# A two-layer hybrid encoder trunk on one core: the eight gate features computed with the tokens as the stationary side

## Chip, cores and metric

One Trainium2 chip, one core. The metric is the device time of one execution in microseconds (us).

## What is computed

The input x is 512 tokens by 1024 features in float32. Layer 0 normalises x (RMSNorm), projects it with one weight matrix and feeds two groups of heads: four gated DeltaNet heads and four differential-attention heads. Layer 1 is a banded attention. Each layer ends with a gated MLP. The part that the change touches is the projection of the DeltaNet gates: two numbers per head and token, a and b, so eight columns of the weight matrix in all.

```
h = rmsnorm(x, even_norm_mix[e])
dn_qkv, dn_a, dn_b, dn_gate, fq, fk, fv = split_cols(h @ even_w_in[e], IN0_SPLITS)
...
beta = jax.nn.sigmoid(b)
g = -jnp.exp(A_log) * jax.nn.softplus(a + dt_bias)
```

The recurrence of the DeltaNet needs beta and the running sums of g in every chunk, so nothing of the DeltaNet past its convolutions can start before them.

## The kernel before, in words

Every large product is made in a split form. A float32 operand is written as head plus tail, both in the float32r type: ScalarE rounds it to the head (`wh` for a weight, `mh` for the normalised input without its token scale), VectorE subtracts to get the tail (`wl`, `ml`). A product is then three matmuls, head by head, tail by head and head by tail, which add up in PSUM. The 1024 features are eight blocks of 128 (KD = 8), the 512 tokens four blocks of 128 (NB = 4). In the generator `features` (line 668 issues the matmul) a 128x128 block of a weight is stationary and all 512 tokens move past it; eight blocks times three forms, 24 matmuls, make one tile of 128 output features, and two tiles are one unit: tile 0 and tile 1 of slot 0 (banks acc0, acc1), then of slot 1 (acc2, acc3).

The first unit of each slot feeds DeltaNet heads 0 and 1. TensorE's order around the change is written out by hand: half of tile 0, the row sums of the norm (`norm_rows`), and so on, three matmuls at each step of `run`. Before the change it is: tile 0 and tile 1 of slot 0; `ab_features`; tile 0 of slot 1; `ab_tokens`; tile 1 of slot 1; then `dn_pair(0, ...)`, which begins with sums over the squares of q and k (`token_sums`, line 690) and later mixes its own small matmuls with further units.

`ab_features` computes the gate features as rows: for each of the eight blocks, three matmuls (`mm3`, lines 625 to 627) with a stationary side of 128x8 (`abh`, `abl`) and 512 moving tokens, into rows 0 to 7 of bank R2. VectorE copies these rows to SBUF (line 1785, into a slice of the tile U of head 1, which the profile calls dn_U). `ab_tokens` turns the rows into columns by four transposes (line 735) into bank R3: tokens on the partitions, eight features per token block. VectorE then multiplies by the token scale `rcol` (line 1798, `abz`) and begins a chain of small steps, in which each waits for the one before it (`chain`, lines 1802 to 1819), with five small ScalarE steps between (lines 1290 to 1295). They end in `gall` (g) and `ball` (beta).

VectorE works through its own list in a fixed order too: the convolutions of q and k of head 0 (lines 1519 to 1531), the copy of line 1785, the two halves of a weight tail (line 1540, after ScalarE's head, line 390), the gate chain, the convolutions of q and k of head 1, again a weight tail, and then the start of `dn_pair`. Each convolution begins by reading its finished tile (`tile_full`), so q of head 1 needs tile 0 of slot 1 and k of head 1 needs tile 1 of slot 1.

Of the kernel before, what the change touches and what calls it, by code (L numbers as in the profile page):

```python
# [25 lines left out]
F32 = mybir.dt.float32  # L26
R32 = mybir.dt.float32r
ALU = mybir.AluOpType
ACT = mybir.ActivationFunctionType

P = 128
S = 512
NB = S // P
D = 1024
KD = D // P
# [69 lines left out]
                                                  ("t31", 3), ("pv", 3)]  # L105
XT_JOBS = [(f"x{k}", k % 4) for k in range(KD)]
NORM_JOBS = [("col", 1), ("row", 0)]
AB_JOBS = [("abT", 2), ("ab", 3)]


class Bank:
# [19 lines left out]
BANK.phase("xt", XT_JOBS, 1)  # L131
BANK.phase("ab", AB_JOBS, 1)
BANK.phase("norm0", NORM_JOBS[1:], 1)
# [33 lines left out]
def build(nc, T, out):  # L167

    ctx = ExitStack()
    with ctx:  # L170
        def sb(name, shape, dt=F32, where=ctx):
            return where.enter_context(nc.sbuf_tensor(name, shape, dt))
# [3 lines left out]
        def sem(name):  # L176
            if name not in sems:
                sems[name] = ctx.enter_context(nc.semaphore(name))
            return sems[name]
# [13 lines left out]
        mh = sb("mh", [P, KD, S], R32)  # L193
        ml = sb("ml", [P, KD, S], R32)
# [3 lines left out]
        cst = sb("cst", [P, C_WIDTH])  # L198
# [13 lines left out]
        rcol = sb("rcol", [P, NB])  # L212
# [9 lines left out]
        abz = sb("abz", [P, NB, 8], F32, ctx)  # L222
# [6 lines left out]
        nq = sb("nq", [P, 2, NB], F32, ctx)  # L229
        sub8 = sb("sub8", [P, 1])  # L230
        abw = sb("abw", [P, KD, 8])
        abh = sb("abh", [P, KD, 8], R32)
        abl = sb("abl", [P, KD, 8], R32)
        sb("line2", [P, LINE])

        def cblk(n):
# [14 lines left out]
        start = ExitStack()  # L251
# [8 lines left out]
        d = [{}, {}]  # L260
# [23 lines left out]
            vn.append(sb(f"vn{h}", [P, P], F32, mix))  # L284
            st.append(sb(f"st{h}", [P, P], F32, mix))
        mix.close()
        abs_ = d[1]["U"][0:8, :]
        mixer = ExitStack()
        oh = sb("oh", [P, KD, S], R32, mixer)
        ol = sb("ol", [P, KD, S], R32, mixer)  # L290
# [56 lines left out]
        def full(eng, phase, job, i):  # L347

            b, n = BANK.use(phase, job, i)
            eng.wait_ge(sem(f"R{b}_full"), n + 1)  # L350
            return R[b]

        def free(ins, phase, job, i):

            b, _ = BANK.use(phase, job, i)
            ins.then_inc(sem(f"R{b}_read"), 1)

        def read(eng, phase, job, i):

            b, n = BANK.use(phase, job, i)  # L360
            eng.wait_ge(sem(f"R{b}_read"), n + 1)
# [251 lines left out]
        def _(pe):  # L613
            def job(phase, name, i, first=True):
                b, n = BANK.use(phase, name, i)
                if not (isinstance(n, int) and n == 0):
                    pe.wait_ge(sem(f"R{b}_read"), n)
                return R[b]

            def done(ins, phase, name, i):  # L620
                b, _ = BANK.use(phase, name, i)
                ins.then_inc(sem(f"R{b}_full"), 1)

            def mm3(o, ah_, al_, bh_, bl_, first, last):
                nc.tensor.matmul(o, ah_, bh_, start=first, stop=False)
                nc.tensor.matmul(o, ah_, bl_, start=False, stop=False)
                return nc.tensor.matmul(o, al_, bh_, start=False, stop=last)

            HEADS = (True, True)

            def features(s, g, mov, tiles=2, kn=KD, norm=None, ready=None, halves=None):
# [46 lines left out]
            def both(a, b):  # L678
                yield from a
                yield from b  # L680

            def run(gen, n=1000):
                for _ in range(n):
                    if next(gen, 0) == 0:
                        return
# [23 lines left out]
            for k in range(KD):  # L709
                r = job("xt", f"x{k}", 0)  # L710
                for b in range(NB):
                    last = nc.tensor.transpose(r[:, b * P:(b + 1) * P], xin[:, b, k * P:(k + 1) * P], ident)
# [5 lines left out]
            for t, n in ((1, 110), (2, 66)):  # L718
                last = nc.tensor.transpose(acc[1][:, t * P:t * P + n], prow[0:n, t, :], cst[0:n, 0:n])
            last.then_inc(sem("pv_full"), 1)  # L720

            def ab_features():

                pe.wait_ge(sem("ab_split"), 1)
                r = job("ab", "abT", 0)
                for k in range(KD):
                    last = mm3(r[0:8, :], abh[:, k, :], abl[:, k, :], mh[:, k, :], ml[:, k, :], k == 0, k == KD - 1)
                done(last, "ab", "abT", 0)

            def ab_tokens():  # L730

                read(pe, "ab", "abT", 0)
                r = job("ab", "ab", 0)
                for b in range(NB):
                    last = nc.tensor.transpose(r[:, b * 8:b * 8 + 8], abs_[:, b * P:(b + 1) * P], cst[0:8, 0:8])
                done(last, "ab", "ab", 0)


# [324 lines left out]
            first = both(features(0, 0, (mh, ml), norm=0), features(1, 0, (mh, ml)))  # L1063
            run(first, KD)
            pe.wait_ge(sem("cst_rest"), 16)
            norm_rows(0)
            run(first, KD)
            ab_features()
            run(first, KD)
            ab_tokens()  # L1070
            run(first)

# [28 lines left out]
            first = both(features(0, UNIT["odd"], (mh, ml), norm=2), features(1, UNIT["odd"], (mh, ml), tiles=1))  # L1101
# [22 lines left out]
            for k in range(KD):  # L1124
                r = job("yt", f"x{k}", 0)
                pe.wait_ge(sem("x_gain"), k + 1)
                for b in range(NB):
                    last = nc.tensor.transpose(r[:, b * P:(b + 1) * P], x[:, k, b * P:(b + 1) * P], ident)
# [4 lines left out]
        def _(act):  # L1133
            A = nc.scalar.activation
# [49 lines left out]
                A(mh[:, k, :], xs[:, k, :], ACT.Copy, scale=pv[:, k:k + 1]).then_inc(sem("m_head"), 1)  # L1184
            units_split_act(act, 1, 0)
            act.wait_ge(sem("abw_in"), 16)
            A(abh[:, :, :], abw[:, :, :], ACT.Copy).then_inc(sem("ab_head"), 1)


            def silu(i, c, dst):  # L1190
# [93 lines left out]
            first = qk_evac(0)  # L1284
# [175 lines left out]
        def _(dve):  # L1460
            V = nc.vector
# [24 lines left out]
            for k in range(KD):  # L1486
                r = full(dve, "xt", f"x{k}", 0)
# [8 lines left out]
            for t, n in ((1, 110), (2, 66)):  # L1496
                ins = V.tensor_copy(pv[:, t * P:t * P + n], acc[1][:, t * P:t * P + n])  # L1497
            ins.then_inc(sem("pv_copied"), 1)
            for k in range(1, KD):
# [1 line left out]
            norm_rstd(0)  # L1501
            units_split_dve(dve, 1, 0)
            dve.wait_ge(sem("ab_head"), 1)
            V.tensor_tensor(abl[:, :, :], abw[:, :, :], abh[:, :, :].bitcast(F32), ALU.subtract)\
                .then_inc(sem("ab_split"), 1)
            dve.wait_ge(sem("pv_copied"), 2)
            V.tensor_scalar(sub8[:, :], pv[:, PV_SUB:PV_SUB + 1], 1.0 - LAM_INIT, None, ALU.mult).then_inc(step, 1)
# [37 lines left out]
            def qk_evac(p):  # L1545
                for h in (0, 1):
                    for c in (0, 1):
                        yield conv(2 * p + h, c, 0)
                        yield conv(2 * p + h, c, 1)
                    yield from half_splits(h, 2 * p + 1)  # L1550
# [230 lines left out]
            first = qk_evac(0)  # L1781
            for _ in range(4):
                next(first, 0)
            r = full(dve, "ab", "abT", 0)
            free(V.tensor_copy(abs_[:, :], r[0:8, :]), "ab", "abT", 0)
            for _ in range(2):
                next(first, 0)

# [2 lines left out]
            def chain(ins):  # L1791
                n_step[0] += 1
                ins.then_inc(step, 1)
                dve.wait_ge(step, n_step[0])


            r = full(dve, "ab", "ab", 0)
            ins = V.tensor_tensor(abz[:, :, :], r[:, 0:NB * 8].rearrange("p (b n) -> p b n", n=8),
                                  rcol[:, :].unsqueeze(2).broadcast_to([P, NB, 8]), ALU.mult)
            free(ins, "ab", "ab", 0)  # L1800
            read(dve, "ab", "ab", 0)
            chain(V.tensor_tensor(abt[0][:, :, :], abz[:, :, 0:4], dtb[:, :].unsqueeze(1).broadcast_to([P, NB, NH]),
                                  ALU.add))
            chain(V.tensor_tensor(lt[:, :, :], lp[:, :].rearrange("p (a b n) -> p a b n", a=2, b=2)[:, :, 0, :],
# [238 lines left out]
            for k in range(KD):  # L2043
                r = full(dve, "yt", f"x{k}", 0)
# [27 lines left out]
```

## Time and profile before

| | |
|---|---|
| median of 3 runs | 1423.88 us |
| lowest and highest run | 1422.25 and 1428.67 us |
| the profiled execution's own time | 1423.34 us |
| its span in the trace | 1421.7 us |
| TensorE (PE) busy | 1365.0 us, 96% of the span |
| TensorE weight loads (PEld) busy | 1120.1 us, 79% |
| VectorE (DVE) busy | 827.9 us, 58% |
| ScalarE (ACT) busy | 582.4 us, 41% |
| GpSimd (POOL) busy | 131.9 us, 9% |
| mean granted TensorE clock | 0.981 of full |

The profiled execution ran 1.6 us longer than its span, which lies around the traced instructions. The busy share is an average over stages with different limits: it says that TensorE works nearly always, not that a given matmul sets the end. For a change in one place the chain of waits and the timeline of that place decide. A timeline row gives start, length, engine, line, operation, and in brackets the idle time before it and what ended it. Lengths of matmuls overlap, so the pace of a stream is read from the starts of its rows.

### The profile page before, as it was taken

Reading aid. Unit: us, or ns where it says so; the run is one execution under the profiler, and the core shown is the slowest. Engines: PE = TensorE matmul, PEld = TensorE weight load, DVE = VectorE, ACT = ScalarE, POOL = GpSimd, SP = SyncE. Lnnn points to the kernel's source line nnn. Section 1 sums busy time; section 2 is a strip of 40 time slices with the busy share of each in tenths; the row PEclk is TensorE's granted clock in tenths of the full one; section 3 lists DMA queues with packets and bytes.
Section 4 is the critical chain, followed back from the end, with each engine's and each line's share of the span. In section 5 each row is a group of like instructions: output and inputs, shape, how many; then the busy total and the mean of one; then the engine's idle time right before and its main releaser. Section 6 shows DMA issues by size and latency. Waiting matters only on the chain.

```text
span 1421.7 us, 19249 instructions
## 1 busy us (share of the span) xinstructions
PE 1365.0 (96%) x6871; PEld 1120.1 (79%) x6871; DVE 827.9 (58%) x1243; ACT 582.4 (41%) x804; POOL 131.9 (9%) x141
## 2 busy tenths in 40 slices
PE   5799999999899999999999999999999999999996
PEld 4689889777678888888888777777878888888885
DVE  5685685677475665345655555555655654355543
ACT  4423322355444443223334455554435442233342
POOL 1050040011041100000001100100210000000011
PEclk9899899999999999999999999999999999999998
DMA  7411110124144533343223432233223333433132
GB/s 205 139 30 30 45 27 19 45 60 129 35 128 132 164 101 89 96 118 89 77 74 104 113 88 73 72 91 100 59 81 97 90 94 89 114 93 110 55 93 59
DMA packets 218643, 124.77 MB, mean 88 GB/s; under 512 B 6047, under 2 KB 215434, under 8 KB 218340
## 3 DMA queue, kind: packets, MB, share of 16 engines
q1 hardware_dynamic: 213744, 112.48, 28.1%
q0 software_dynamic: 3664, 11.58, 2.9%
q8 instruction: 31, 0.51, 0.2%
q10 hardware_dynamic: 1188, 0.08, 0.1%
q14 instruction: 16, 0.13, 0.0%
HBM read 119.87 MB, written 9.48 MB: 91 GB/s over the span
## 4 chain that ended last, share of the span: by engine, by line
PE 92%; DVE 4%; ACT 2%; DMA 1%; issue 1%; SPq 0%; POOL 0%; DVEq 0%; ACTq 0%; POOLq 0%
PE acc L668 73%; PE R L784 5%; PE acc L1029 3%; PE R L898 2%; PE R L912 2%; PE R L1002 1%; PE R L690 1%; DVE wl L394 1%; PE R L782 1%; PE R L772 1%; ACT wh L390 1%; PE R L961 1%; DMA xin<-in_x 1%; DVE cta L1531 1%; DVE ml L1481 1%
## 5 line engine op out<-in xcount | busy, mean ns | idle before, releaser
L668 PE MATMUL acc<-mh,wh 128*128 128x512 f32 x1120 | 318.1, 404 | 5.4 <-DVE pv L1497 4.6
L668 PE MATMUL acc<-ml,wh 128*128 128x512 f32 x1120 | 308.6, 393 | 3.1 <-DVE ml L1481 3.1
L668 PE MATMUL acc<-mh,wl 128*128 128x512 f32 x1120 | 308.2, 394 | 0.0
L394 DVE TENSOR_TENSOR wl<-raw,wh 128x2048 fp32r<-128x2048 f32 (+1 forms) x104 | 224.4, 2157 | 118.2 <-ACT wh L390 118.2
L390 ACT ACTIVATE wh<-raw 128x2048 fp32r<-128x2048 f32 x112 | 202.5, 1808 | 130.2 <-PE acc L668 128.8
L668 PEld LDWEIGHTS acc<-mh,wh 128*128 128x128 f32 x1120 | 205.9, 189 | 57.2 <-issue 15.7
L668 PEld LDWEIGHTS acc<-ml,wh 128*128 128x128 f32 x1120 | 209.4, 189 | 48.8 <-DVE ml L1481 4.6
L668 PEld LDWEIGHTS acc<-mh,wl 128*128 128x128 f32 x1120 | 210.4, 189 | 43.4
L529 POOL TENSOR_TENSOR ssum<-ssum,sq 128x512 f32<-128x512 f32 x32 | 49.9, 1560 | 733.5 <-ACT sq L1143 732.9
L1993 DVE SCALAR_TENSOR_TENSOR cta<-cb,pv,cta 128x512 f32<-128x512 f32 x88 | 66.2, 752 | 74.1 <-ACT cta L1420 67.7
L668 PE MATMUL acc<-ah,wh 128*128 128x512 f32 x352 | 95.4, 389 | 0.0
L668 PE MATMUL acc<-al,wh 128*128 128x512 f32 x352 | 95.4, 389 | 0.0
L668 PE MATMUL acc<-ah,wl 128*128 128x512 f32 x352 | 95.4, 389 | 0.0
L1420 ACT ACTIVATE cta<-cb,pv 128x512 f32<-128x512 f32 x44 | 35.9, 817 | 103.8 <-DVE cb L1986 103.6
L668 PEld LDWEIGHTS acc<-ah,wh 128*128 128x128 f32 x352 | 66.1, 188 | 13.7
L668 PEld LDWEIGHTS acc<-al,wh 128*128 128x128 f32 x352 | 66.1, 188 | 13.7
L668 PEld LDWEIGHTS acc<-ah,wl 128*128 128x128 f32 x352 | 66.1, 188 | 13.7
L2013 DVE TENSOR_TENSOR x<-x,acc 128x512 f32 (+1 forms) x32 | 22.0, 688 | 70.6 <-PE acc L668 69.9
L1426 ACT ACTIVATE ah<-pd 128x512 f32 x44 | 27.8, 632 | 69.6 <-DVE pd L2002 69.6
L2004 DVE TENSOR_TENSOR al<-pd,ah 128x512 f32 x44 | 30.5, 692 | 44.3 <-ACT ah L1426 44.3
L1424 ACT ACTIVATE sl<-cta 128x512 f32<-128x512 f32 x44 | 27.8, 632 | 64.8 <-DVE cta L1993 64.8
L1842 DVE CUSTOM_DVE_ANT_0 odd_ns<-R,gb 128x128 f32<-128x128 f32 (+3 forms) x64 | 28.8, 487 | 37.3 <-PE R L898 37.3
(308 smaller groups left out, 1624.1 us busy)
## 6 DMA issues: line engine op xcount, KB each, us to landing
raw<-in_ffn_w_in SPq DMA_DIRECT2D x88, 512.0 KB, 5.0
raw<-in_even_w_in SPq DMA_DIRECT2D x24, 512.0 KB, 5.3
raw<-in_ffn_w_out SPq DMA_DIRECT2D x32, 384.0 KB, 4.1
raw<-in_ffn_w_out SPq DMA_DIRECT2D x32, 320.0 KB, 3.7
raw<-in_odd_w_qkv SPq DMA_DIRECT2D x16, 512.0 KB, 4.5
rel_bias_extended<-rel_bias_rows POOLq DMA_DIRECT2D x16, 320.0 KB, 4.0
raw<-in_even_w_out SPq DMA_DIRECT2D x8, 512.0 KB, 4.6
raw<-in_odd_w_qkv SPq DMA_DIRECT2D x16, 256.0 KB, 3.1
```

The source lines that it names most:

```text
L390: nc.scalar.activation(wh[s][:, 0:n], raw[s][:, 0:n], ACT.Copy).then_inc(sem(f"w_head{s}"), 1)
L394: nc.vector.tensor_tensor(wl[s][:, 0:n], raw[s][:, 0:n], wh[s][:, 0:n].bitcast(F32), ALU.subtract).then_inc(sem(f"w_tail{s}"), 1)
L529: pool.tensor_tensor(ssum[:, :], ssum[:, :], sq[s][:, :], ALU.add).then_inc(sem("ssum"), 1)
L668: last = nc.tensor.matmul(acc[2 * s + t][:, :], ws[0 if form[0] else 1][:, t, k, :], mov[0 if form[1] else 1][:, k, :], start=form == HEAD ...
L784: last = nc.tensor.matmul(r[:, t], a[:, t], triu if b is triu else b[:, t], start=True, stop=True)
L898: ins = nc.tensor.matmul(r[m][:, w], qs[x_][half[m], b * P:(b + 1) * P], ks[y][half[m], w], start=(step == 0), stop=(step == 2))
L912: last = nc.tensor.transpose(r[:, c0 + k * P:c0 + (k + 1) * P], src[:, k * P:(k + 1) * P], ident)
L1029: ins = nc.tensor.matmul(acc[2 * s + t][:, :], ws[0 if form[0] else 1][:, t, k, :], (oh if form[1] else ol)[:, k, :], start=form == HEADS ...
L1420: A(cta[s][:, :], cb[s][:, ALPHA - 2:ALPHA - 2 + S], ACT.Identity, bias=pv[:, bass.ds(j + (PV_CB + JF * layer), 1)], scale=pv[:, bass.ds(j ...
L1842: free(V.tensor_tensor_reduce(out=dst[t % 2][:, 0:w], in0=R[t % 2][:, 0:w], in1=bias, scale=-1.0, scalar=3e38, op0=ALU.add, op1=ALU.min, a ...
L1993: V.scalar_tensor_tensor(out=cta[s][:, :], in0=cb[s][:, o:o + S], scalar=pv[:, bass.ds(j + (w0 + JF * tap), 1)], in1=cta[s][:, :], op0=ALU ...
L2004: V.tensor_tensor(dyn(al, 2 * i + s), pd[s][:, :], dyn(ah, 2 * i + s).bitcast(F32), ALU.subtract).then_inc(sem("a_tail"), 1)
```

## The change

The stationary and the moving side are swapped. A 128x128 block of `mh` or `ml` (128 features by 128 tokens) is stationary, and the weight columns move: the head and the tail of the eight columns stand side by side in one tile `abx` of 16 columns per block. `mh` takes all 16 (head by head and head by tail at once, into two groups of 8 columns of PSUM), `ml` the first 8. This gives 4 token blocks x 8 feature blocks x 2 = 64 matmuls with the tokens on the partitions already, so the copy of line 1785 and the four transposes go. The two groups of columns are added on VectorE. `ab_features` is gone, and `ab_tokens` stands where it stood, ahead of tile 0 of slot 1.

```diff
-AB_JOBS = [("abT", 2), ("ab", 3)]
+AB_JOBS = [("ab", 3)]
...
-        abh = sb("abh", [P, KD, 8], R32)
-        abl = sb("abl", [P, KD, 8], R32)
+        abx = sb("abx", [P, KD, 16], R32)
...
-            def ab_features():
-
-                pe.wait_ge(sem("ab_split"), 1)
-                r = job("ab", "abT", 0)
-                for k in range(KD):
-                    last = mm3(r[0:8, :], abh[:, k, :], abl[:, k, :], mh[:, k, :], ml[:, k, :], k == 0, k == KD - 1)
-                done(last, "ab", "abT", 0)
-
             def ab_tokens():
 
-                read(pe, "ab", "abT", 0)
+                pe.wait_ge(sem("ab_split"), 1)
+                pe.wait_ge(sem("m_tail"), KD)
                 r = job("ab", "ab", 0)
                 for b in range(NB):
-                    last = nc.tensor.transpose(r[:, b * 8:b * 8 + 8], abs_[:, b * P:(b + 1) * P], cst[0:8, 0:8])
+                    t = slice(b * P, (b + 1) * P)
+                    for k in range(KD):
+                        nc.tensor.matmul(r[:, b * 16:b * 16 + 16], mh[:, k, t], abx[:, k, :],
+                                         start=(k == 0), stop=False)
+                        last = nc.tensor.matmul(r[:, b * 16:b * 16 + 8], ml[:, k, t], abx[:, k, 0:8],
+                                                start=False, stop=(k == KD - 1))
                 done(last, "ab", "ab", 0)
...
             run(first, KD)
-            ab_features()
-            run(first, KD)
             ab_tokens()
             run(first)
...
-            r = full(dve, "ab", "abT", 0)
-            free(V.tensor_copy(abs_[:, :], r[0:8, :]), "ab", "abT", 0)
...
             r = full(dve, "ab", "ab", 0)
-            ins = V.tensor_tensor(abz[:, :, :], r[:, 0:NB * 8].rearrange("p (b n) -> p b n", n=8),
-                                  rcol[:, :].unsqueeze(2).broadcast_to([P, NB, 8]), ALU.mult)
+            parts = r[:, 0:NB * 16].rearrange("p (b a n) -> p b a n", a=2, n=8)
+            chain(V.tensor_copy(abz[:, :, :], parts[:, :, 0, :]))
+            ins = V.tensor_tensor(abz[:, :, :], abz[:, :, :], parts[:, :, 1, :], ALU.add)
             free(ins, "ab", "ab", 0)
             read(dve, "ab", "ab", 0)
+            chain(V.tensor_tensor(abz[:, :, :], abz[:, :, :], rcol[:, :].unsqueeze(2).broadcast_to([P, NB, 8]), ALU.mult))
```

ScalarE writes the head into `abx[:, :, 0:8]` in place of `abh`, and VectorE the tail into `abx[:, :, 8:16]` in place of `abl`, each at the same place in its list.

TensorE's list around the gate features, before the change (acc are the tiles of the projection, R the bank of the gate features; the second number of a stationary or output shape is the moving side's columns):

```order
L668 MATMUL acc<-ml,wh 128x512 x4
L625 MATMUL R<-mh,abh 8x512
L626 MATMUL R<-ml,abh 8x512
L627 MATMUL R<-mh,abl 8x512
...
L668 MATMUL acc<-mh,wh 128x512 x4
...
L735 MATMUL R<-cst,dn_U 128x8 x4
L668 MATMUL acc<-mh,wh 128x512 x4
```

And after it:

```order
L661 MATMUL acc<-ml,wh 128x512 x4
L723 MATMUL R<-abx,mh 128x16
L725 MATMUL R<-abx,ml 128x8
...
L661 MATMUL acc<-mh,wh 128x512 x4
L661 MATMUL acc<-ml,wh 128x512 x4
L661 MATMUL acc<-mh,wl 128x512 x4
```

The pair of lines 723 and 725 comes 32 times in a row where the triple of lines 625 to 627 came 8 times; the transposes that stood between tile 0 and tile 1 of slot 1 are gone.

VectorE's list from the last convolution of head 0 to the start of the gate chain, before:

```order
L1531 SCALAR_TENSOR_TENSOR cta<-cb,pv,cta 128x512 x3
L1785 COPY dn_U<-R 8x512
L1540 TENSOR_TENSOR wl<-raw,wh 128x1024 x2
L1798 TENSOR_TENSOR abz<-R,rcol 128x32
L1802 TENSOR_TENSOR abt<-abz,dtb 128x16
```

And after:

```order
L1520 SCALAR_TENSOR_TENSOR cta<-cb,pv,cta 128x512 x3
L1529 TENSOR_TENSOR wl<-raw,wh 128x1024 x2
L1786 COPY abz<-R 128x32
L1787 TENSOR_TENSOR abz<-abz,R 128x32
L1790 TENSOR_TENSOR abz<-abz,rcol 128x32
L1791 TENSOR_TENSOR abt<-abz,dtb 128x16
```

One instruction of 512 columns is gone ahead of the weight tail, and one instruction has become three behind it. Nothing else changes its place.

## Rows read from the trace of the kernel before

**Rows 1.** The page: busy time of TensorE, and the chain that ended last.
```profile
PE 1365.0 (96%) x6871; PEld 1120.1 (79%) x6871; DVE 827.9 (58%) x1243; ACT 582.4 (41%) x804; POOL 131.9 (9%) x141
...
PE 92%; DVE 4%; ACT 2%; DMA 1%; issue 1%; SPq 0%; POOL 0%; DVEq 0%; ACTq 0%; POOLq 0%
```

**Rows 2.** The chain in order of time (start us, us, what), around the gates.
```profile
46.02 0.36 PE R L735 x4
...
51.62 0.70 DVE cb L1519
...
55.30 0.70 DVE cb L1519
...
62.55 2.36 DVE wl L1540 x2
...
65.37 2.08 PE R L784 x8
```

**Rows 3.** Timeline of TensorE, 34.9 to 60.8 us (start, length, engine, line).
```profile
34.88 0.40 PE L625 MATMUL R<-mh,abh 128*8 128x512 f32 x1
...
40.42 1.07 PE L668 MATMUL acc<-mh,wh 128*128 128x512 f32 x4
...
45.95 0.41 PE L735 MATMUL R<-cst,dn_U 8*128 8x8 f32 x4
...
50.96 1.07 PE L668 MATMUL acc<-mh,wl 128*128 128x512 f32 x4
51.87 0.94 PE L690 MATMUL R<-cst,dn_sqq 128*128 128x1 f32 x8
...
60.77 1.87 PE L690 MATMUL R<-cst,dn_sqq 128*128 128x1 f32 x8 [7.07 <-ACT dn_sqk L1206]
```

**Rows 4.** Timeline of VectorE, 40.6 to 46.8 us.
```profile
40.62 0.68 DVE L1785 COPY dn_U<-R 8x512 f32<-8x512 f32 x1 [0.65 <-PE R L627]
43.66 2.36 DVE L1540 TENSOR_TENSOR wl<-raw,wh 128x1024 fp32r<-128x1024 f32 x2 [2.36 <-ACT wh L390]
46.40 0.19 DVE L1798 TENSOR_TENSOR abz<-R,rcol 128x32 f32<-128x32 f32 x1 [0.38 <-PE R L735]
46.62 0.17 DVE L1802 TENSOR_TENSOR abt<-abz,dtb 128x16 f32<-128x16 f32 x1
```

**Rows 5.** Timeline of TensorE at two stretches of one moving column per 128x128 stationary side.
```profile
172.13 3.55 PE L690 MATMUL R<-cst,dn_A 128*128 128x1 f32 x16
175.55 2.05 PE L784 MATMUL R<-cst,dn_decT 128*128 128x128 f32 x8
...
272.71 1.84 PE L690 MATMUL R<-cst,dn_A 128*128 128x1 f32 x16
274.48 0.33 PE L898 MATMUL R<-ksh,qsh 64*128 64x128 f32 x2
```

**Rows 6.** Stretches: length, busy us of PE, PEld, DVE, ACT, POOL, then granted clock, DMA.
```profile
168.70:175.50 6.80, 6.80 (x32) 6.80 (x33) 4.92 (x12) 4.76 (x7) 0.00 (x0) 0.50 0.21 49
...
34.90:40.40 5.50, 5.50 (x25) 2.19 (x24) 4.79 (x7) 1.03 (x2) 0.00 (x0) 1.00 1.13 395
21.40:24.80 3.40, 3.40 (x8) 2.75 (x9) 3.40 (x6) 3.38 (x5) 0.00 (x0) 0.50 1.03 268
54.00:55.40 1.40, 0.00 (x0) 0.00 (x0) 1.26 (x3) 0.17 (x1) 0.00 (x0) 1.00 0.00 0
55.60:60.70 5.10, 0.00 (x0) 0.00 (x0) 3.13 (x5) 2.02 (x5) 0.00 (x0) 0.50 0.00 0
...
69.00:69.50 0.50, 0.50 (x5) 0.50 (x5) 0.47 (x2) 0.00 (x0) 0.00 (x0) 0.80 1.19 289
```

**Rows 7.** Timeline of TensorE, the first wide matmuls after a pause, at the lower clock.
```profile
21.39 2.02 PE L668 MATMUL acc<-mh,wh 128*128 128x512 f32 x4 [4.57 <-DVE pv L1497]
23.21 1.84 PE L668 MATMUL acc<-mh,wl 128*128 128x512 f32 x4
24.88 1.09 PE L668 MATMUL acc<-ml,wh 128*128 128x512 f32 x4
```

More of the change, by code:

```diff
@@ L286, in build @@
         mix.close()
-        abs_ = d[1]["U"][0:8, :]
         mixer = ExitStack()
@@ L622, in done @@
                 ins.then_inc(sem(f"R{b}_full"), 1)
[L624 to L627, printed above, removed]
             HEADS = (True, True)
@@ L720, in _, with ab_tokens @@
             last.then_inc(sem("pv_full"), 1)
-            def ab_features():
+            def ab_tokens():
                 pe.wait_ge(sem("ab_split"), 1)
-                r = job("ab", "abT", 0)
-                for k in range(KD):
-                    last = mm3(r[0:8, :], abh[:, k, :], abl[:, k, :], mh[:, k, :], ml[:, k, :], k == 0, k == KD - 1)
-                done(last, "ab", "abT", 0)
-            def ab_tokens():
-                read(pe, "ab", "abT", 0)
+                pe.wait_ge(sem("m_tail"), KD)
                 r = job("ab", "ab", 0)
                 for b in range(NB):
-                    last = nc.tensor.transpose(r[:, b * 8:b * 8 + 8], abs_[:, b * P:(b + 1) * P], cst[0:8, 0:8])
+                    t = slice(b * P, (b + 1) * P)
[4 more added lines that the diff above has]
+                                                start=False, stop=(k == KD - 1))
                 done(last, "ab", "ab", 0)
@@ L1186, in _ @@
             act.wait_ge(sem("abw_in"), 16)
-            A(abh[:, :, :], abw[:, :, :], ACT.Copy).then_inc(sem("ab_head"), 1)
+            A(abx[:, :, 0:8], abw[:, :, :], ACT.Copy).then_inc(sem("ab_head"), 1)
             def silu(i, c, dst):
@@ L1503, in _ @@
             dve.wait_ge(sem("ab_head"), 1)
-            V.tensor_tensor(abl[:, :, :], abw[:, :, :], abh[:, :, :].bitcast(F32), ALU.subtract)\
+            V.tensor_tensor(abx[:, :, 8:16], abw[:, :, :], abx[:, :, 0:8].bitcast(F32), ALU.subtract)\
                 .then_inc(sem("ab_split"), 1)
```

## Prediction

> **What bounds the kernel now.** I read the page first: TensorE is busy 96% of the span and carries 92% of the chain that ended last [rows 1]. So a microsecond taken from TensorE counts in most places, and I next asked whether it counts here. The chain in order of time [rows 2] shows TensorE until the four transposes end at 46.38, and then VectorE and ScalarE: the gate chain, the two convolutions of head 1 (51.62 and 55.30), a weight tail at 62.55, and TensorE again only at 65.37. The timeline of TensorE [rows 3] agrees: after the last wide matmul, issued before 51.87, and sixteen one-column ones it sits idle for 7.07 us until 60.77. So TensorE's work between 35 and 53 us is bound only through the places where VectorE waits for it. From the dense part behind 65 us on TensorE leads, so a delay of VectorE here comes out whole at the end.
>
> The timeline of VectorE [rows 4] shows how thin the first of these places is. The copy of line 1785 ends at 41.30, and VectorE then idles 2.36 us until ScalarE's weight head arrives. The weight tail ends at 46.02, and the gate chain begins at 46.40, 0.38 us later, released by the transposes. So all that TensorE and the copy do for the gates before the change costs the end 0.38 us.
>
> **What goes.** On TensorE 24 matmuls of 512 columns, from 34.88 to 40.42, are 5.5 us, and the four transposes, 45.95 to about 46.3, are 0.4 us [rows 3]. On VectorE the copy of 0.68 us lies in idle time [rows 4] and is worth nothing; without it VectorE would idle from 40 to 43.66 for the same weight head. ScalarE's list is the same. No DMA moves: the loads of SyncE wait for weight tails, and these keep their time.
>
> **What comes on VectorE.** Three small instructions in a row where one was. One step of this kind, with the wait for its forerunner, is 0.22 us by the starts 46.40 and 46.62 [rows 4]. If the gates are in PSUM in time, the first starts at 46.02, and line 1791 would start at 46.02 + 3 x 0.22 = 46.68, against 46.62 for the same step before: 0.06 us later. The 0.38 us won are given back. The new order puts the gates' bank ahead of tile 0 of slot 1, so this needs the 64 matmuls to end before 46.0. The new wait for the eight `m_tail` costs nothing: those tails were needed by the tiles ahead, long done.
>
> **What comes on TensorE.** 64 matmuls, each with its own 128x128 stationary side and 16 or 8 moving columns. The trace has no float32r matmul of this shape. The nearest rows are the sums of line 690, also a 128x128 stationary side each time, with one moving column: 16 of them take 274.48 - 272.71 = 1.77 us, 0.111 us each, at the upper clock, and 175.55 - 172.13 = 3.42 us, 0.214 us each, at the lower one [rows 5]. The bound above is the wide stream itself, which swaps such a side for each matmul: four take 51.87 - 50.96 = 0.91 us, 0.228 each at the upper clock [rows 3]. I take line 690's prices, since the shape is almost the same: 64 x 0.111 = 7.1 us, against 5.5 + 0.4 removed, or 64 x 0.214 = 13.7 us. One matmul costs half of a wide one, but there are 64 for 24.
>
> For the loads a rule speaks against the change in the same size. The Trainium skill, "TensorE: Matmul & The Clock Gate", section "LDWEIGHTS (loading the stationary operand)", prices a load by its columns over 1.2: 107 ns for 128 columns, so an estimate of 6.8 us for 64, and 7 ns for 8 columns. The trace's 0.111 us agrees; the sum does not use the page's figure.
>
> **The clock.** This decides the sign. Which price holds hangs on the granted clock. In the stretch 168.70 to 175.50 TensorE is busy all of 6.80 us with one-column matmuls, and the clock stands at 0.50, the lower level (1.2 GHz), throughout [rows 6]: this work did not lift it. After the last wide matmul before 51.87 the clock was still 1.00 (the upper level, 2.4 GHz) until 55.4 and 0.50 from 55.6 on, and the first 1.8 us of that were one-column matmuls [rows 3, 6]. The removed block, 34.90 to 40.40, ran at 1.00 [rows 6] because it was itself wide. I therefore expect the clock to fall inside the new block. Where, the rows leave open; I take half of the matmuls at each level: 32 x 0.111 + 32 x 0.214 = 10.4 us, with 7.1 and 13.7 as the ends.
>
> The wide matmuls behind it then start low. After the pause at 21.39 the first eight took 24.88 - 21.39 = 3.49 us, 0.436 each [rows 7], 0.21 more than at the upper clock. Eight of them cost 1.7 us.
>
> **The sum.** Block from 34.9 to 45.3. Gates in time for 46.0. Tile 0 of slot 1, 24 wide matmuls, 5.5 + 1.7 = 7.2 us, to 52.5; the convolution of q of head 1 wants it at 51.6 and starts 1.0 us late. Tile 1, 5.5 us, to 58.0, its end 0.1 later. The convolution of k of head 1 wanted it at 55.30 [rows 2], and with q's delay alone would start at 56.3; it starts at 58.1, **2.8 us late**. Behind it stand, on VectorE and ScalarE one after the other, the silu, the squares, ScalarE's weight head, the weight tail at 62.55 and the first work of the pair at 65.37; all of them move by it. Against the profiled execution's 1423.3 this gives 1426.1. That execution is 0.5 us below the median of the three runs. The ends: with 7.1 us the block ends at 42.0 and tile 1 at 53.1, before 55.3, so nothing is late and the time is 1423.3 (the 0.06 us of VectorE is below what can be seen). With 13.7 us it ends at 48.6, the gates are late by 2.3 us, tile 1 ends at 61.4, and k's convolution is 6.1 us late: 1429.4. The clock rises again only at about 69 [rows 6], with the path on TensorE since 65.37; if that rise shifts, it may add or take 1 to 2 us (at half speed, 3.8 us of work would shrink by 1.9).
>
> A difference under 0.5%, 7.1 us, is what a measurement of this kernel hardly tells from none. All of this lies inside it.
>
> **Rival 1: the clock holds (chance 0.35).** The block takes 7.1 us at 1.00, TensorE's idle time before 60.77 shrinks by 1.2 us, and the end is where it was: 1423.3. For it speaks that TensorE is never without work in the block, and that 16 moving columns are more than one. Against it stands the stretch from 168.70 [rows 6]. The Trainium skill, same page, section "Why this matters for your kernels", advises to keep TensorE busy to reach and hold the upper clock; by that rule the clock holds here and the time is that of this rival. The trace disagrees where the work is one-column matmuls: busy 6.80 of 6.80 us at 0.50.
>
> **Rival 2: a float32r side is not swapped faster than the wide stream shows (chance 0.05, of it 0.04 for the slow form).** The wide rows never show a swap below 0.228 us at the upper and 0.436 at the lower clock, since the 512 columns cover it; line 690's sides are of float32 in two passes and could differ. With half of the matmuls at each clock the block takes 32 x 0.228 + 32 x 0.436 = 21.2 us and ends at 56.1, tile 1 at 68.9, and k's convolution is 13.6 us late: 1436.9, slower than before beyond doubt. With the clock up throughout, 14.6 us, tile 1 ends at 60.6: 1428.6. With the clock low behind the block, the loss passes 7.1 us when tile 1 ends after 62.4, so when the block ends after 49.6: 14.7 us, or 0.230 us for one matmul on average. Against it: weight loads of the wide stream and of line 690 look alike in length, and nothing in the rows ties a swap to the type.
>
> **Rival 3: TensorE leaves the chain and the end comes earlier (chance 0.05, of it 0.01 beyond 0.5%).** The chain lists the 24 matmuls and the transposes, some 5.9 us, and whoever reads only that list expects them back. The 0.38 us of [rows 4] is all that can come before the weight tail holds, and the two added steps take 0.44. The time would be 1423.3 - 0.3 = 1423.0 if the steps overlap better than their starts say; with the pair's start at the upper clock too, 1.9 less, 1421.1.
>
> **How the numbers follow.** My forecast, a clock that falls in the block, has a chance of 0.55, and its own range is 1423.5 to 1429.5. The range reaches down over rivals 1 and 3 to 1422.0, the price of a run's spread below 1423.3 (the lowest of the three was 1422.25), and up to the end with all 64 at the lower clock. Slower by over 0.5% needs rival 2's slow form, 0.04. Faster by over 0.5% has 0.01. The rest, 0.95, is within it.
>
> **What would show it.** In the trace of the changed kernel: 64 matmuls starting near 34.9, their pace 0.11 us and, from some point on, 0.21; the granted clock 0.50 by the end of the block; the next wide matmuls at 0.44 for some three microseconds; the copy of line 1786 starting near 46.0, ended by no wait for TensorE; the convolution of k of head 1 waiting for TensorE for about 2 us and starting near 58; the idle time of TensorE before the squares of head 1 still about 6 to 7 us; and the first work of the pair (line 784 in the kernel before) near 68 in place of 65.4. The prediction is wrong in its main step if the clock stays at 1.00 through the block, if the pace at the upper clock is not near 0.11, or if k's convolution does not wait for tile 1. It would be wrong as a whole if a delay there did not come out at the end, so if a later stall shrank by it.

## Result, and the profile after

The changed kernel took 1432.51 us in the median of 8 runs (1423.91 to 1434.01), the kernel before 1425.43 us in 8 runs (1421.23 to 1430.66). The ratio is 1.0050, 95% interval 1.0030 to 1.0069: slower, by 7.1 us in the medians, where 2.8 us were forecast and a range up to 1429.5. Both kernels spread over some 10 us. Between executions of one kernel the time goes with the mean granted clock of TensorE: of the kernel before, executions at 0.983 took 1421 to 1423 us and those at 0.976 to 0.977 about 1428 to 1430 (by the 98 runs of it beside the experiments). The changed kernel has such a split too: seven of its eight runs took 1430.8 to 1434.0 us at 0.972 to 0.975, and one took 1423.91 us at 0.980.

The page of the profiled execution (span 1431.3 us, against 1421.7) shows that TensorE is busy 12.9 us longer while VectorE and ScalarE do the same as before [rows 1]:

```profile
span 1431.3 us, 19321 instructions
PE 1377.9 (96%) x6907; PEld 1134.7 (79%) x6907; DVE 828.5 (58%) x1244; ACT 582.3 (41%) x804; POOL 132.0 (9%) x141
```

The timeline of TensorE through the block and behind it answers to [rows 3, 7]. The columns are start, length, engine, line, what, shapes:

```profile
30.34 1.02 PE L696 MATMUL R<-sq,cst 128*128 128x512 f32 x2
...
36.69 0.17 PE L723 MATMUL R<-abx,mh 128*128 128x16 f32 x1
...
37.05 0.26 PE L723 MATMUL R<-abx,mh 128*128 128x16 f32 x1
37.16 0.25 PE L725 MATMUL R<-abx,ml 128*128 128x8 f32 x1
...
43.56 0.36 PE L723 MATMUL R<-abx,mh 128*128 128x16 f32 x1
43.77 0.35 PE L725 MATMUL R<-abx,ml 128*128 128x8 f32 x1
...
46.12 2.05 PE L661 MATMUL acc<-mh,wh 128*128 128x512 f32 x4
47.97 1.91 PE L661 MATMUL acc<-ml,wh 128*128 128x512 f32 x4
49.68 1.88 PE L661 MATMUL acc<-mh,wl 128*128 128x512 f32 x4
51.39 1.10 PE L661 MATMUL acc<-mh,wh 128*128 128x512 f32 x4
```

The pace is 0.11 us at first and 0.21 us later. The block takes 46.12 - 36.69 = 9.4 us, with about 40 of the 64 matmuls at the fast pace and 24 at the slow one. The twelve wide matmuls behind it take 5.27 us in place of 2.7, 2.5 us more. This execution had already been 1.8 us later at the row sums of the norm (line 696, in the kernel before line 703 at 28.54), ahead of anything the change touches. The kernels below whose lists are as before up to there start it anywhere between 28.5 and 30.6, so I count from this row on.

The granted clock (third number from the end, as in [rows 6]) says the same:

```profile
36.70:41.10 4.40, 4.40 (x42) 4.40 (x40) 4.12 (x7) 0.63 (x1) 0.00 (x0) 1.00 1.12 364
41.20:46.10 4.90, 4.90 (x25) 4.90 (x25) 1.22 (x2) 4.24 (x5) 0.00 (x0) 0.50 0.62 264
46.20:51.30 5.10, 5.10 (x13) 4.03 (x13) 3.58 (x11) 1.84 (x6) 1.98 (x5) 0.50 0.49 128
...
69.90:78.60 8.70, 8.70 (x33) 7.93 (x34) 5.66 (x15) 3.65 (x9) 0.00 (x0) 0.50 0.48 121
78.70:100.00 21.30, 21.30 (x108) 16.84 (x107) 17.08 (x24) 4.60 (x5) 9.57 (x7) 1.00 0.00 1
```

It is 1.00 for the first 4.4 us of the block and 0.50 for the rest and for the first wide matmuls. The last two rows belong to the first pair, to which I come back.

The timeline of VectorE, against [rows 4], and the convolutions of head 1 against [rows 2]:

```profile
45.45 2.36 DVE L1529 TENSOR_TENSOR wl<-raw,wh 128x1024 fp32r<-128x1024 f32 x2 [3.68 <-ACT wh L388]
47.73 0.18 DVE L1786 COPY abz<-R 128x32 f32<-128x32 f32 x1
47.95 0.19 DVE L1787 TENSOR_TENSOR abz<-abz,R 128x32 f32<-128x32 f32 x1
48.17 0.19 DVE L1790 TENSOR_TENSOR abz<-abz,rcol 128x32 f32<-128x32 f32 x1
48.40 0.17 DVE L1791 TENSOR_TENSOR abt<-abz,dtb 128x16 f32<-128x16 f32 x1
...
54.39 0.69 DVE L1508 TENSOR_TENSOR cb<-acc,rstd 128x512 f32<-128x512 f32 x1 [0.81 <-PE acc L661]
...
59.77 0.69 DVE L1508 TENSOR_TENSOR cb<-acc,rstd 128x512 f32<-128x512 f32 x1 [1.81 <-PE acc L661]
```

The copy starts as the weight tail ends, without a wait; the gate chain's first own step (line 1791) stands at 48.40, and less the 1.8 us this is 46.60, where it was 46.62. Tile 0 of slot 1 comes 0.8 us late and tile 1 another 1.8. In the kernel before both waits were absent. TensorE's pause before the squares of head 1, 7.07 us before the change [rows 3], is now 3.83 us:

```profile
65.25 1.87 PE L683 MATMUL R<-cst,dn_sqq 128*128 128x1 f32 x8 [3.83 <-ACT dn_sqk L1195]
```

**The ledger.** The start of the same TensorE instructions in the two profiled executions, and their difference. The first work of pair 0 in the kernel before is the 65.37 of [rows 2]:

| place | before | after | difference |
|---|---|---|---|
| row sums of the norm | 28.54 | 30.34 | +1.80 |
| pair 0, first work (line 784, now 775) | 65.37 | 69.85 | +4.48 |
| pair 0, first spread (line 772, now 763) | 72.74 | 79.56 | +6.82 |
| pair 1, first work | 175.55 | 182.27 | +6.72 |
| pair 1, first spread | 184.07 | 192.07 | +8.00 |
| sums behind pair 1 (line 690, now 683) | 272.71 | 280.71 | +8.00 |
| values of the first attention head (line 907, now 898) | 281.07 | 290.69 | +9.62 |
| span | 1421.7 | 1431.3 | +9.6 |

So 1.8 us is the later start, 2.7 us is what the block does by way of VectorE, and 2.3, 1.3 and 1.6 us come at three later places where the code is the same. In all three the clock is low in the changed kernel where it was up before. Before, it had risen at 69.00 to 69.50 [rows 6]; after, at 78.7. At the last of them it falls once more:

```profile
282.96 1.62 PE L661 MATMUL acc<-mh,wh 128*128 128x512 f32 x4
284.38 1.91 PE L661 MATMUL acc<-ml,wh 128*128 128x512 f32 x4
286.09 1.48 PE L661 MATMUL acc<-mh,wl 128*128 128x512 f32 x4
```

The same three rows in the kernel before started at 274.96, 275.98 and 276.88, so twelve wide matmuls took 4.4 us here and 2.8 us there. These are differences of two single executions, 1432.98 and 1423.34 us; the medians are 7.1 us apart.

### The profile page after: what moved, and what is told of

Same layout as the page of the kernel before. It is cut to its first block, busy times and chain, and to the rows that moved or that the text cites. A ratio compares the mean times of both kernels' runs of the same rounds, so it can differ in the third digit from the quotient of the medians.

```text
span 1431.3 us, 19321 instructions
## 1 busy us (share of the span) xinstructions
PE 1377.9 (96%) x6907; PEld 1134.7 (79%) x6907; DVE 828.5 (58%) x1244; ACT 582.3 (41%) x804; POOL 132.0 (9%) x141
## 4 chain that ended last, share of the span: by engine, by line
PE 93%; DVE 3%; ACT 2%; DMA 1%; issue 1%; SPq 0%; POOL 0%; DVEq 0%; ACTq 0%; POOLq 0%
PE acc L661 73%; PE R L775 5%; PE acc L1020 3%; PE R L889 2%; PE R L903 2%; PE R L993 1%; PE R L683 1%; PE R L773 1%; PE R L763 1%; ACT wh L388 1%; PE R L952 1%; DMA xin<-in_x 1%; DVE wl L392 1%; DMA out<-ob 0%; PE R L878 0%
## 5 line engine op out<-in xcount | busy, mean ns | idle before, releaser
L661 PE MATMUL acc<-ml,wh 128*128 128x512 f32 x1120 | 312.4, 397 | 3.1 <-DVE ml L1470 3.1
```

Source lines behind the costliest of these rows:

```text
L661: last = nc.tensor.matmul(acc[2 * s + t][:, :], ws[0 if form[0] else 1][:, t, k, :], mov[0 if form[1] else 1][:, k, :], start=form == HEAD ...
```

## Experiments

Two questions. Is it the clock that makes the block long (theory A) or the 64 loads (B)? And are the 4 to 5 us behind the first pair chance (L), a fixed price of a later start (P, G), or a price that depends on where the start falls (Q)? Each kernel ran beside the kernel before on the same chip. Experiments 1 to 4, 5 to 8 and 9 to 12 are three groups, with their own runs of the kernel before (medians 1423.72, 1423.37 and 1423.74 us). The ratio with its 95% interval is an estimate of its own and not the quotient of the two medians. With these spreads the two can differ: in experiment 7 the medians are 3.0 us apart, while the ratio of 1.0004 is 0.6 us. So 2 or 3 us between medians are not much to build on. "Pair start" is the first work of pair 0 (line 784 of before) minus the row sums of the norm, 36.83 us in the kernel before and 39.51 in the changed one. It comes from one profiled execution, the time from the medians.

**1. Passing the columns eight times.**

```diff
-nc.tensor.matmul(r[:, b * 16:b * 16 + 16], mh[:, k, t], abx[:, k, :], ...)
+nc.tensor.matmul(r[:, b * P:(b + 1) * P], mh[:, k, t],
+                 abx[:, k, :].unsqueeze(1).broadcast_to([P, 8, 16]), ...)
...
```

The matmul of `ml` gets its 8 columns eight times over in the same way.

> The changed kernel, with the same 64 stationary loads, but the 16 (and 8) weight columns are passed eight times over, so that 128 (and 64) columns move past each load; the gate features come out eight times and one set is read. Theory A (the block's narrow matmuls let the clock fall, and the fall is the price): the granted clock stays 1.00 from 34 us to 55 us, the pace is 0.11 us for each of the 64, the block takes 7.1 us, k's convolution of head 1 waits for no matmul, and the median is within 2 us of the kernel before. Theory B (the 64 loads themselves are the price): the block still runs at 0.15 us or more on average, 9.4 us or more, and the time stays 5 us or more above before.

1431.57 against 1423.72 us, ratio 1.0053 (1.0037 to 1.0069): no better. The clock was not held:

```profile
35.10:38.50 3.40, 3.40 (x33) 3.40 (x31) 3.19 (x5) 0.63 (x1) 0.00 (x0) 1.00 1.19 362
38.60:45.30 6.70, 6.70 (x34) 6.70 (x33) 2.96 (x4) 4.86 (x5) 0.52 (x1) 0.50 0.59 253
```

Half of the block again ran at 0.50, with 128 and 64 columns behind each load. My expectation was wrong: eight times the columns did not save it. It does not speak for B, since the loads at 1.00 kept a pace of 0.11 us; it says that this remedy does not reach the clock.

The profiled execution of this kernel took 1423.67 us, the fastest of its twelve. It is worth a look, because its delay is that of the changed kernel: k's convolution waits 1.81 us and the pair start is 39.54. But here the clock rises at 72.7, 4.4 us after the pair's first work, where it was 8.8 us in the changed kernel's profile:

```profile
68.28 2.07 PE L778 MATMUL R<-cst,dn_decT 128*128 128x128 f32 x8 [1.03 <-DVE dn_decT L1636]
...
73.08 1.17 PE L661 MATMUL acc<-mh,wh 128*128 128x512 f32 x4
74.09 1.08 PE L661 MATMUL acc<-ml,wh 128*128 128x512 f32 x4
```

Counted from the row sums, its first attention head comes 3.1 us later than in the kernel before; in the changed kernel's profile that was 7.8 us. (By its end this execution is level with the kernel before's profiled one, which was low from 424.2 to 427.5 us where this one was not.) So the same delay brings some 5 us more behind it in one execution and almost nothing in another. Of the 32 runs of the changed kernel and of experiments 1 and 9, which share its delay, seven took 1423.3 to 1426.9 us and the others 1430.8 to 1434.3.

**2. The block in four groups.**

```diff
 for b in range(NB):
     ...16 matmuls of token block b...
+    if b == NB - 1:
+        done(last, "ab", "ab", 0)
+    run(first, 2)
```

> The changed kernel, its 64 matmuls in four groups of 16 with 6 wide matmuls behind each. Theory A: wide matmuls never stop for more than 1.8 us, the clock stays 1.00, tile 0 of slot 1 ends at 35+7.1+5.5 = 47.5 us and tile 1 at 53, before k's convolution wants it; time as before, within 2 us. Theory B: 2.7 us or more above before, as in the changed kernel.

```profile
36.80:54.90 18.10, 18.10 (x113) 16.15 (x112) 11.26 (x27) 8.79 (x13) 1.91 (x5) 1.00 0.69 225
```

The clock stays 1.00 through all 64, their 7.1 us and the 48 wide matmuls among and behind them. k's convolution waits for nothing (57.76, right behind q's). The pair start is 37.36, 0.53 us later than before, because the last group ends just late for the gate chain, which waits 0.27 us and has two more steps. The median is 1425.82, 2.1 us above before, ratio 1.0011 (0.9995 to 1.0026): just at the 2 us of theory A and not told from no difference. So A holds for the block: the same 64 loads, with the clock up, cost VectorE 0.5 us in place of 2.7.

**3. Half of the block.** Only `mh` is stationary; the tail of the input is left out of the gate features.

```diff
-nc.tensor.matmul(r[:, b * 16:b * 16 + 8], ml[:, k, t], abx[:, k, 0:8], ...)
```

> The changed kernel without the 32 matmuls of ml: the tail of the input is left out of the gate features. Theory A: 32 narrow matmuls take 3.6 us at 0.111 us, end before the clock falls or just as it falls; tile 1 of slot 1 ends near 50 to 51 us and k's convolution waits for nothing, so the time is within 1 us of before if nothing else moves. If the clock still falls, behind the block, the wide matmuls pay 1.7 us but tile 1 is ready at 52: still no wait.

```profile
35.23 3.63 PE L723 MATMUL R<-abx,mh 128*128 128x16 f32 x32
38.72 1.80 PE L661 MATMUL acc<-mh,wh 128*128 128x512 f32 x4
40.32 1.91 PE L661 MATMUL acc<-ml,wh 128*128 128x512 f32 x4
```

32 matmuls in 3.5 us, and the clock falls just behind them. The wide matmuls pay for it, yet tile 1 is in time, the pair start is 36.93 and the median 1423.88 against 1423.72 (0.9988 to 1.0021). A low clock where TensorE has slack was free here.

**4 to 6. A later pair start and nothing else.** The kernel before, with extra VectorE work ahead of k's convolution of head 1:

```diff
+for late in (d[0]["U"], d[1]["U"], d[0]["A2"], d[1]["A2"], ...)[:n]:   # n is 2, 4 or 6
+    V.tensor_tensor(late, rstd[:, :], rstd[:, :], ALU.mult)
```

Four instructions:

> The kernel before, with four extra VectorE instructions (about 2.5 us, results unused) ahead of k's convolution of head 1, so the first pair starts about 2.5 us later and TensorE's matmuls are all as before. The changed kernel's profiled run lost 2.7 us there and 5.1 us more at three later places, where the clock rose later or fell once more. Theory L (the later losses are chance of the execution): median 2 to 3 us above before. Theory P (a later start of the pair by itself brings the later rises): median 5 to 8 us above before.

Six:

> The kernel before with six extra VectorE instructions (about 3.7 us) ahead of k's convolution of head 1, in place of the four (2.4 us) that cost 8.2 us. Theory Q (the extra loss depends on where the pair's start falls against the moments at which the clock can change, and a few microseconds more bring it past the bad place): the median is lower than that of four, 4 to 6 us above before. Theory G (any later start costs its own length and some 6 us more): 9 to 10 us above before.

Two:

> The same with two extra instructions (about 1.2 us). Theory Q: a mix of executions like before and executions 5 us or more longer, median 1.5 to 5 us above before. Theory G: 7 us above before. Theory L (no extra loss): 1.2 us above.

| extra instructions | pair start | later than before | median | above before | ratio, interval |
|---|---|---|---|---|---|
| 2 | 37.97 | 1.1 | 1428.93 | 5.6 | 1.0031 (1.0017 to 1.0045) |
| 4 | 39.26 | 2.4 | 1431.88 | 8.2 | 1.0057 (1.0040 to 1.0074) |
| 6 | 40.62 | 3.8 | 1427.47 | 4.1 | 1.0023 (1.0008 to 1.0038) |

A delay of 2.4 us on VectorE alone, every matmul in its old place and order, cost 8.2 us (in six runs, all between 1430.48 and 1432.52): as much as the changed kernel's whole loss, 7.1 us in the result and 7.6 and 7.9 in experiments 9 and 1. And 3.8 us of delay cost 4.1. L and G fall for the medians, and the idea of Q stands: the loss is the delay plus 0.3 to 5.8 us, not in proportion to it, and more delay can cost less. Q's own number for two instructions, 1.5 to 5 us, was missed at 5.6. Experiment 1 adds that chance of the execution has a part too, since at one and the same delay a run can pay the extra or not. The profiles show where it lies. With four instructions, stretches of TensorE:

```profile
57.90:69.20 11.30, 3.57 (x16) 3.49 (x16) 7.48 (x13) 6.00 (x8) 0.00 (x0) 0.50 0.00 1
69.30:78.20 8.90, 8.90 (x33) 8.13 (x34) 5.70 (x16) 3.85 (x9) 0.00 (x0) 0.50 0.47 120
78.30:100.00 21.70, 21.70 (x109) 17.18 (x109) 17.59 (x25) 4.45 (x5) 10.06 (x8) 1.00 0.00 1
```

With six:

```profile
71.00:75.30 4.30, 4.28 (x20) 4.28 (x21) 3.40 (x10) 0.60 (x1) 0.00 (x0) 0.50 0.88 233
75.40:100.00 24.60, 24.60 (x125) 19.68 (x124) 20.28 (x32) 7.83 (x12) 10.48 (x8) 1.00 0.01 2
```

With four, the pair's first work starts at 69.30 and the clock rises at 78.2, 8.9 us later, with all of it on TensorE's path. With six it starts at 71.03 and the clock rises at 75.4, 4.4 us later. In the kernel before it was 3.8 us, in the changed kernel, with 69.85 and 78.7, 8.8 us: the changed kernel behaves as the one with four instructions does, whose delay is nearly the same (2.4 and 2.7 us). The one profile with two instructions, 1426.27 us long and the second fastest of its twelve runs, has the rise 3.7 us after the pair start, as before the change; what the median of 1428.93 lost beyond 1.1 us is in no trace.

**7 and 8. Keeping TensorE busy in the pause.** 20 wide matmuls into an unused bank ahead of the squares of head 1 and 10 behind them; results unused. A wait for the bank stands ahead of them and is left out here.

```diff
...
+for _ in range((20, 10)[h]):
+    nc.tensor.matmul(R[2][:, :], mh[:, 0, 0:P], mh[:, 0, :], start=True, stop=True)
```

> The kernel before, with 20 wide matmuls into an unused bank in TensorE's pause before the squares of head 1 and 10 more behind these squares (results unused), so that TensorE is not left with one-column matmuls and waiting there. If the clock's fall at the first pair and its late rise are the loss: the granted clock stays 1.00 from 30 us to 100 us, the pair's first work at 65.4 runs at full pace, and the median is 2 to 3 us below before, with less spread. If the pair's clock does not matter: as before, or slower by what the added matmuls delay.

> The changed kernel with the same 30 added matmuls. Its block still lets the clock fall at 38 to 41 us and k's convolution is still late by 2.7 us. If the rest of its loss is the pair's low clock: 2 to 4 us above the kernel before with the same matmuls, about level with the kernel before itself. If the rest is elsewhere: still 7 us above before.

In the kernel before: 1426.33 against 1423.37, ratio 1.0004 (0.9987 to 1.0021), so no gain, where 2 to 3 us were expected if the low clock at the pair were the loss. In its profile the clock stayed up through the pause but still fell, from 65.4 to 68.8 us, under the ten matmuls behind the squares. They took 4.06 us in place of 2.3 and pushed the pair's first work back:

```profile
62.95 1.05 PE L690 MATMUL R<-cst,dn_sqq 128*128 128x1 f32 x8 [2.46 <-ACT dn_sqk L1210]
63.86 1.03 PE L690 MATMUL R<-cst,dn_sqk 128*128 128x1 f32 x8
64.76 4.06 PE L807 MATMUL R<-mh 128*128 128x512 f32 x10
68.61 1.16 PE L784 MATMUL R<-cst,dn_decT 128*128 128x128 f32 x8
```

The pair then ran at full pace (1.16 us for eight where it was 2.08), but the start was 38.00, 1.2 us later, and this profiled execution, 1424.8 us long, was low again at 277 to 280 us, where the kernel before's was not. In the changed kernel the clock stayed up through the pause and the pair; yet its median is 1429.06 us, ratio 1.0033 (1.0017 to 1.0049): 5.7 us above the kernel before, where about level with it was expected if the rest were the pair's low clock, and 2.7 us above the kernel before with the same matmuls, or 4.1 us by the two ratios. The two pair starts, 39.73 and 38.00, are 1.7 us apart. Whether an extra loss is left between the two is not resolved by this. What it shows is that the low clock at the first pair is not all of the loss. Both results can be fitted into Q and do not single out one later place.

**9. Extra work inside the changed kernel's wait.** Two of the same instructions ahead of k's convolution in the changed kernel.

> The changed kernel with two extra VectorE instructions (1.2 us) ahead of k's convolution of head 1. There VectorE waits 1.8 us for tile 1 of slot 1, so 1.2 us of extra work should fit into that wait and move nothing. Expected by both theories: as the changed kernel, 7 to 9 us above before. If instead it comes out lower by over 2 us, the changed kernel's loss varies from session to session by more than I believe.

```profile
56.25 1.29 DVE L1813 TENSOR_TENSOR dn_U<-rstd 128x512 f32<-128x512 f32 x2
58.15 0.69 DVE L1508 TENSOR_TENSOR cb<-acc,rstd 128x512 f32<-128x512 f32 x1 [0.61 <-PE acc L661]
```

The wait of 1.81 us shrinks to 0.61, the pair start is 39.54 (39.51 without), and 1431.32 us is 7.6 above before, ratio 1.0039 (1.0017 to 1.0061). So tile 1 is what k's convolution waits for, and the extra work fits into that wait.

**10 to 12. Other orders.** In 10, q's convolution of head 1 goes ahead of the gate chain, k's between its two halves. In 11 both tiles of slot 1 go ahead of the gates on TensorE as well:

```diff
-            run(first, KD)
-            ab_features()
-            run(first, KD)
-            ab_tokens()
             run(first)
+            ab_features()
+            ab_tokens()
...
-            first = qk_evac(0)
-            for _ in range(4):
-                next(first, 0)
+            for c in (0, 1):
+                conv(0, c, 0)
+                conv(0, c, 1)
+            conv(1, 0, 0)
+            conv(1, 0, 1)
+            for _ in half_splits(0, 1):
+                pass
+            conv(1, 1, 0)
+            conv(1, 1, 1)
             r = full(dve, "ab", "abT", 0)
...
+            for _ in half_splits(1, 1):
+                pass
             dve.wait_ge(sem("ab_e"), 5)
```

ScalarE's exponentials stand behind both heads to match. 12 is the same order with the changed kernel's block.

> The kernel before with VectorE's list changed: the convolution of q of head 1 ahead of the gate chain and k's between its two halves, ScalarE's silu of q ahead of the gates' exponentials; TensorE's list is as before. VectorE then waits for tile 1 of slot 1 (ready at 52) instead of for the gates. The pair's first work starts 3 us earlier, near 62.2. Theory Q: the clock's extra loss may change either way with that shift; median 1 to 6 us below before.

> The kernel before with both tiles of slot 1 ahead of the gate features on TensorE, and VectorE's and ScalarE's lists to match: both convolutions of head 1 first, the second weight tail inside the gate chain. VectorE's idle time from 40 to 43.7 us is filled, the gates run beside the pause. The pair's first work starts near 58.5 in place of 65.4, 7 us earlier. Median 4 to 9 us below before.

> The same order with the changed kernel's 64 narrow matmuls in place of the wide ones, the copy and the transposes. The block runs from 46 to 53 us at the upper clock or to 55.4 if the clock falls in it; the wide form has its gates ready at 52.7. So the narrow form starts its pair 0.5 to 3 us later than e11, and is 0 to 4 us slower than e11; 3 to 7 us below before.

| kernel | pair start | against 36.83 | median (before 1423.74) | ratio, interval |
|---|---|---|---|---|
| 10 | 33.74 | -3.1 | 1419.94 | 0.9971 (0.9952 to 0.9990) |
| 11 | 30.41 | -6.4 | 1417.13 | 0.9952 (0.9934 to 0.9970) |
| 12 | 34.81 | -2.0 | 1423.38 | 0.9982 (0.9964 to 1.0001) |

Kernel 11 is 6.6 us below the kernel before, and its pair starts 6.4 us earlier. It does so by filling VectorE's idle time. In the kernel before VectorE did nothing but the copy of 0.68 us from 39.97 to 43.66 [rows 4]; it waited 2.09 us for ScalarE in the gate chain, and 3.67 us for ScalarE's head ahead of the weight tail at 62.55. In kernel 11 q's convolution stands in the first stretch and the weight tail in the second, and the third is gone; its waits left between head 0's convolutions and the first work of the pair are 0.55, 1.64, 0.50 and 0.27 us. In its profile k's convolution starts at 47.02 and the gates run beside TensorE's pause:

```profile
41.25 0.69 DVE L1513 TENSOR_TENSOR cb<-acc,rstd 128x512 f32<-128x512 f32 x1 [0.55 <-PE acc L668]
...
47.02 0.68 DVE L1513 TENSOR_TENSOR cb<-acc,rstd 128x512 f32<-128x512 f32 x1
...
52.23 0.68 DVE L1785 COPY dn_U<-R 8x512 f32<-8x512 f32 x1 [1.64 <-PE R L627]
53.41 0.19 DVE L1796 TENSOR_TENSOR abz<-R,rcol 128x32 f32<-128x32 f32 x1 [0.50 <-PE R L735]
```

Here the gates are on the path, and the two forms can be compared. In kernel 12 VectorE waits for the block:

```profile
56.73 0.19 DVE L1785 COPY abz<-R 128x32 f32<-128x32 f32 x1 [6.67 <-PE R L725]
```

Its gates are ready 56.73 - 28.56 = 28.2 us after the norm's row sums, against 53.41 - 29.27 = 24.1 us in kernel 11, copy and transposes included, and the time is 6.3 us more. The expectation was 0 to 4 us more, and 3 to 7 us below before where it came out 0.4 below: missed on both counts. The 4.1 us are not the loads alone. The clock was 0.50 again from 48.9 us on in this block, which took 10.8 us where 64 loads at 0.11 us are 7.1, and it rose only at 72.7.

## Why the prediction was wrong

**Right, and nearly to the number:** that the clock falls inside the block (10.4 us forecast with half of the matmuls at either clock, 9.4 measured with 40 and 24; 0.111 and 0.214 us the pace, 0.11 and 0.21 measured); that the wide matmuls behind it start low (1.7 us forecast for eight, 2.5 measured for twelve); that VectorE's three steps give back the 0.38 us (0.06 late forecast, 0.02 early measured); that k's convolution is the one that waits (1.81 us); and the delay at the pair's first work, 2.8 us forecast and 2.7 measured. That this last number is so close is in part luck: the block was 1.0 us shorter than forecast and the wide matmuls cost 0.8 us more, and the two nearly cancel. One sign was given wrongly: TensorE's pause before the squares of head 1 was to stay at 6 to 7 us and shrank to 3.83. The forecast's own terms give 7.07 - (10.4 - 5.9) - 1.7 + 2.8 = 3.7 us, so this was a slip and not a fault of the mechanism. Of the clock in the block the trace of before had told enough: the one-column stretch at 0.50 [rows 6] was a fair model.

**The step that failed** is the end of the sum: "all of them move by it" and "it may add or take 1 to 2 us". Of the median's 7.1 us, 2.7 are this delay by the profile, and the rest, 4.4, comes behind it. I had seen that the clock rises only near 69 us with the path on TensorE, and bounded a shift of that rise by 1 to 2 us at one place. In the profiled execution it cost 2.3 us there, 1.3 at the second pair and 1.6 behind it, 5.2 us in all, and the kernel with four extra VectorE instructions shows that a delay of this size brings this by itself (8.2 us for 2.4). It does not bring it in every execution (experiment 1, 1423.67 us). The three extra losses are not independent either: each shifts what follows. My range ended at 1429.5 because I added only what delays the pair and nothing for what the delay does to the clock later. The base had a share in the miss as well: the sum started from one execution of 1423.3 us, and the kernel before came to 1425.43 us over eight runs. From that base 2.8 us more are 1428.2 and the end with all 64 at the lower clock is 1431.5, still below the 1432.51 measured.

**The rivals.** Rival 1, the clock holds, is out for the block as written; it came true only when wide matmuls stood between the groups (experiment 2), and then the time was within 0.5% of before, as priced. The rule cited there from the Trainium skill, "TensorE: Matmul & The Clock Gate", section "Why this matters for your kernels", to keep TensorE busy to reach and hold the upper clock, did not hold here: from 36.70 on TensorE was busy 4.40 of 4.40 us and the clock fell all the same. Rival 2, slow swaps, is out: 0.11 us at 1.00. Rival 3 is out; nothing came earlier.

**The chances.** 0.95 for within 0.5% was far too sure. The ratio's interval of 1.0030 to 1.0069 lies across the bound. The spread of 6 us in three runs of the kernel before (1422.25 to 1428.67) was in front of me, against a claim that nothing here could exceed 7.1 us; a kernel whose own executions differ by that much has places that can be tipped.

**Open.** What fixes at which moment the clock rises within one execution was not tried, and so it stays open why one execution pays the extra loss and another of the same kernel does not. That a delay can bring an extra loss is shown; its size is not understood: the range that Q gave held for six instructions (4.1 us) and not for two (5.6 us). The later places were not each isolated; experiments 7 and 8 changed the first and the others moved too.

## What to carry to other kernels

Swapping sides to save columns does not pay when the number of stationary loads grows more than the price of one falls. Here a narrow matmul with its load costs half of a wide one, 0.11 against 0.23 us, so 64 of them are more than 24 wide ones (7.1 against 5.5 us), and a long row of them can cost the clock for itself and for the wide work behind it. Where such a row is needed, put wide matmuls between its parts, or put it where TensorE has slack. And where an engine's pause makes the clock fall, do not take a small delay ahead of it at face value: delay the start alone, by two or three lengths and with enough runs to see their spread, before explaining a loss; the gain to look for is in what the waiting engine could do meanwhile (6.6 us here, from order alone).

## What the runs showed that I had not expected

A longer delay was cheaper than a shorter one: 3.8 us cost 4.1, while 2.4 cost 8.2. Moving 128 and 64 columns past each load instead of 16 and 8 left the load's pace at 0.11 us and did not keep the clock, which was 0.50 from 38.6 us on. And a clock at 0.50 behind the half block cost nothing that can be measured (1423.88 against 1423.72), because the tiles it slowed were not yet wanted. The changed kernel itself can run as fast as the kernel before: 1423.91 us once in eight.
